# Trunk with a mixture of experts: the fold of the up rows and of the gate rows one half later in each expert pass, with the work that reads them one slot later

## The chip, the cores and the metric

The kernel runs on one core of one Trainium2 chip. The metric is the device time of one execution in microseconds. Its engines are PE (TensorE, matrix products), ACT (ScalarE), DVE (VectorE), POOL (GpSimd) and SP (SyncE, which here only issues the loads of weights). Each engine works off its own list of instructions in order, and they meet at semaphores.

## What is computed

Two layers over 256 rows of 2048 numbers. Each layer is an attention part with three kinds of heads, which the change doesn't touch, and then a mixture of 16 experts, of which each row takes two:

```python
hg = jnp.einsum('nd,edf->nef', t, wg)
hu = jnp.einsum('nd,edf->nef', t, wu)
act = jax.nn.silu(hg) * hu * combine[:, :, None].astype(t.dtype)
out = jnp.einsum('nef,efd->nd', act, wd)
```

For one expert, gate `wg` and up `wu` are 2048 x 512 and down `wd` is 512 x 2048, all in 32-bit floats.

## The kernel before

**Passes.** The experts of a layer are worked off in 16 passes of `step`. Pass k multiplies the gathered rows of expert k by its gate and up weights, and the gated rows of expert k-1 by its down weights. The weights of a pass come as 24 *halves* of 128 x 1024. `PLAN[False]`, written out by hand, is their order: `gggguuggddggdduudduudduu`, halves 0 to 23, g for gate, u for up, d for down. So halves 0 to 7 are gate and up alone, and the first down half is half 8. Pass 0 has no down halves and another order (`PLAN[True]`). After pass 15 come the down halves of the last expert alone.

**A half.** SP loads the weights in pieces of two halves into a ring of 8 buffers (`raw`, and `proj`, which is free in this part). For half h, ACT copies it to a rounded *high* part (`wh`, `cut` on ACT, L555), DVE subtracts this from the half to make the *low* part (`wl`, `cut` on DVE, L1157), and PE multiplies both. `wh` and `wl` have four buffers each (`CUT = 4`), so ACT starts half h only when PE is through with half h-4 (semaphore `cut_free`). A gate or up half is four matrix products on PE (`up_half`, L971 and L973), a down half six (`down_half`, L987 to L989).

**Extra work at slots.** All four engines run the same loop over h, and extra work stands behind the half of a slot: after `cut(h)` on ACT and DVE, after half h on PE. PE is up to four halves behind the cuts, so slot h of ACT and DVE lies earlier in time than slot h of PE. For the up rows of expert k-1, whose last half is half 23 of the pass before, the pass begins with this chain:

- ACT, slot 3 (`UP_OUT`): `up_out` copies the up rows out of their bank (L739).
- PE, slot 1 (`UP_TURN`): `turn_act` folds the two halves of the partitions and turns them, into bank 6 (L962).
- DVE, slot 4: `gated` multiplies them with the gate (L1594).
- ACT, slot 5: `act_hi` makes the high part, two instructions (L744).
- DVE, slot 6: `act_lo` makes the low part (L1600).
- PE: `down_half` of half 8 waits for it.

In between, ACT also stores the last expert's finished rows (`store`, L752), at slots 1, 2, 4 and 6. At slot 6 the store stands behind whatever the slot has of `act_hi`.

The gate rows of expert k have the like chain later in the pass: `gate_out` on ACT at slot 15 (L731), the fold on PE behind half 13 (`GATE_TURN`), `gate_sigmoid` on ACT at slot 17 (L735), `gate_silu` on DVE at slot 19 (L1588). In slots 17 and 22 ACT and DVE also move the turned rows of the next expert (`rows_hi`, L726, and `rows_lo`, L1583).

Of the kernel before, what the change touches and what calls it, by code (L numbers as in the profile page):

```python
# [139 lines left out]
PLAN = {True: "g" * PART + "u" * PART, False: "gggguuggddggdduudduudduu", None: "d" * PART}  # L140
GATED_AT = {first: PLAN[first].rindex("g") for first in (False, True)}
GATE_OUT = {first: at + CUT for first, at in GATED_AT.items()}
GATE_TURN = {first: at + 2 for first, at in GATED_AT.items()}
UP_OUT = CUT - 1
UP_TURN = 1
LAST = NE - 2
JOIN_BANK = (0, 6, 0, 2)
STORE = {PLAN[False].rindex("d") + CUT - 3 * PART + k: n for n, k in enumerate((0, 1, 3, 5))}
# [159 lines left out]
def trunk(nc, x_in, in_units, forget_w, out_units, expert_units, norms, small_in, const_in, router_in,  # L308
          rows_dram, picks_dram, out):
    with ExitStack() as ctx:  # L310
# [231 lines left out]
        def _(e):  # L542
# [6 lines left out]
            def cut(h, slots=RAW, first=0):  # L549

                j = (first + h // 2) % slots
                if h % 2 == 0:
                    e.wait_ge(S[f"raw_landed{j}"], t_.due(f"raw_landed{j}", 16))
                e.wait_ge(S["cut_free"], t_.due("cut_free"))
                act_(wh[:, h % CUT, :], ring[j][:, h % 2 * HALF:(h % 2 + 1) * HALF], ACT.Copy)\  # L555
                    .then_inc(S["hi_ready"], 1)
# [25 lines left out]
            with t_.layers():  # L582
# [141 lines left out]
                def rows_hi(b, g, m=7):  # L724
                    e.wait_ge(S["xt_banked"], t_.due("xt_banked"))
                    act_(stacked[b][:, 8 * g:8 * g + 8, 0:SLOTS],  # L726
                         bank[m][:, :].rearrange("p (c n) -> p c n", n=SLOTS), ACT.Copy).then_inc(S["xt_hi"], 1)

                def gate_out():

                    act_(wide_act, bank[0][:, :], ACT.Copy).then_inc(S["gate_out"], 1)  # L731

                def gate_sigmoid():
                    e.wait_ge(S["gate_turned"], t_.due("gate_turned"))
                    act_(gate_act, bank[6][:, 0:4 * SLOTS], ACT.Sigmoid).then_inc(S["sigmoid"], 1)  # L735

                def up_out():

                    act_(wide_act, bank[1][:, :], ACT.Copy).then_inc(S["up_out"], 1)  # L739

                def act_hi(places=(STACK, 0)):
                    e.wait_ge(S["act_ready"], t_.due("act_ready"))
                    for at in places:
                        ins = act_(actT[:, :, at:at + SLOTS], act.rearrange("p (c n) -> p c n", n=SLOTS), ACT.Copy)  # L744
                    ins.then_inc(S["act_hi"], 1)

                def store(b, k, n):

                    if k == 0:

                        e.wait_ge(S["out_free"], t_.due("out_free"))
                    ins = act_(expert_out[b][:, k * COLS:(k + 1) * COLS], bank[2 + k][0:SLOTS, :], ACT.Copy,  # L752
                               scale=slots[0:SLOTS, bass.ds(n, 1), 2:3].rearrange("p a b -> p (a b)"))
                    if k == 3:
                        ins.then_inc(S["out_ready"], 1)
# [8 lines left out]
                def step(b, k, first=False, last=False, stores=True):  # L764
                    at = 0 if first or b == 1 else 4
                    for h in range(len(PLAN[first])):
                        cut(h, DEEP, at)
                        if h == CUT - 1 and first:
                            for g in range(2):
                                rows_hi(0, g, (7, 5)[g])  # L770
                        if h == UP_OUT and not first:
                            up_out()
                        if h == UP_OUT + 2 and not first:
                            act_hi()
                        if h == GATE_OUT[first]:
                            gate_out()
                        if h == GATE_OUT[first] + 2:
                            gate_sigmoid()
                        if h in XT_MOVE[first] and not last:
                            rows_hi(1 - b, XT_MOVE[first][h])  # L780
                        if h in STORE and stores:
                            store(b, STORE[h], k - 2)
# [27 lines left out]
        def _(e):  # L810
# [147 lines left out]
            def turn_act(at, out, turned):  # L958

                e.wait_ge(S[out], t_.due(out))  # L960
                for k in range(F // P):
                    last = mm(bank[6][:, at + k * SLOTS:at + (k + 1) * SLOTS], wide_act[:, k * P:(k + 1) * P],  # L962
                              cst("fold"), start=True, stop=True)
                last.then_inc(S[turned], 1)
# [27 lines left out]
            def list_slots(experts):  # L992

                if experts[0] in (0, FIRST):
                    e.wait_ge(S["chosen_ready"], t_.due("chosen_ready"))
                for k in experts:
                    for t in range(NT):
                        last = mm(bank[4][0:SLOTS, 4 * k:4 * k + 4], chosen[:, t, k, :], info[:, t, k, :],
                                  start=(t == 0), stop=(t == NT - 1))
                if experts[-1] == NE - 1:  # L1000
                    pair = [chosen[:, t, LAST:NE, :].rearrange("p n s -> p (n s)") for t in range(NT)]
                    for t in range(NT):
                        mm(bank[4][:, 4 * NE:4 * NE + 4], pair[t], info[:, t, NE - 1, :], start=(t == 0),
                           stop=(t == NT - 1))
                    for t in range(NT):
                        last = e.transpose(bank[4][:, (1 + t) * P:(2 + t) * P], pair[t], ident)
                if experts[-1] in (FIRST - 1, NE - 1):
                    last.then_inc(S["slot_banked"], 1)
# [12 lines left out]
            def step(b, first=False, last=False):  # L1021
                for h, part in enumerate(PLAN[first]):
# [5 lines left out]
                    if first and h in LISTED:  # L1028
                        list_slots(LISTED[h])
                    if h == UP_TURN and not first:  # L1030
                        turn_act(4 * SLOTS, "up_out", "up_turned")
                    if h == GATE_TURN[first]:
                        turn_act(0, "gate_out", "gate_turned")
# [115 lines left out]
        def _(e):  # L1149
# [4 lines left out]
            def cut(h, slots=RAW, first=0):  # L1154

                e.wait_ge(S["hi_ready"], t_.due("hi_ready"))
                v.tensor_tensor(wl[:, h % CUT, :],  # L1157
                                ring[(first + h // 2) % slots][:, h % 2 * HALF:(h % 2 + 1) * HALF],
                                wh[:, h % CUT, :].bitcast(F32), ALU.subtract).then_inc(S["lo_ready"], 1)
# [73 lines left out]
            with t_.layers() as layer:  # L1233
# [346 lines left out]
                def rows_lo(b, g, m=7):  # L1580
                    e.wait_ge(S["xt_hi"], t_.due("xt_hi"))
                    k = slice(8 * g, 8 * g + 8)
                    v.tensor_tensor(stacked[b][:, k, SLOTS:STACK], bank[m][:, :].rearrange("p (c n) -> p c n", n=SLOTS),  # L1583
                                    stacked[b][:, k, 0:SLOTS].bitcast(F32), ALU.subtract).then_inc(S["xt_lo"], 1)
# [19 lines left out]
                def choose(a, b):  # L1604
                    v.tensor_tensor(chosen[:, :, a:b, :],
                                    cst("slot").unsqueeze(1).unsqueeze(1).to_broadcast([P, NT, b - a, SLOTS]),
                                    route[:, 3, :, a:b].unsqueeze(3).to_broadcast([P, NT, b - a, SLOTS]),
                                    ALU.is_equal).then_inc(S["chosen_ready"], 1)
# [64 lines left out]
                def step(b, first=False, last=False):  # L1673
                    at = 0 if first or b == 1 else 4
                    for h in range(len(PLAN[first])):
                        cut(h, DEEP, at)
                        if h == CUT - 1 and first:
                            for g in range(2):
                                rows_lo(0, g, (7, 5)[g])
                            choose(FIRST, NE)  # L1680
                        if h == TABLES and first:
                            tables(FIRST, NE)
                            last_tables()
                            ask_again()
                        if h == UP_OUT + 1 and not first:
                            gated()
                        if h == UP_OUT + 3 and not first:
                            act_lo()
                        if h == GATE_OUT[first] + 4:
                            gate_silu()  # L1690
                        if h in XT_MOVE[first] and not last:
                            rows_lo(1 - b, XT_MOVE[first][h])
# [96 lines left out]
```

## Time and profile before

| | before |
|---|---|
| time, three runs | 2103.24, 2096.21, 2102.95 us (median 2102.95) |
| time of the profiled execution | 2098.91 us |
| its span, first to last instruction | 2097.2 us |
| mean granted PE clock over the span | 0.96 |
| busy share of PE, DVE, ACT | 91%, 76%, 69% |
| experts of layer 0 and of layer 1 | about 520 to 1050 us and 1560 to 2097 us |

The span is that of the profiled execution. The shares are means over attention and experts; what one pass of the experts looks like must be read from that stretch alone.

### The profile page before, as it was taken

Reading aid. Unit: us, or ns where it says so; the run is one execution under the profiler, and the core shown is the slowest. Engines: PE = TensorE matmul, PEld = TensorE weight load, DVE = VectorE, ACT = ScalarE, POOL = GpSimd, SP = SyncE. Lnnn points to the kernel's source line nnn. Section 1 sums busy time; section 2 is a strip of 40 time slices with the busy share of each in tenths; the row PEclk is TensorE's granted clock in tenths of the full one; section 3 lists DMA queues with packets and bytes.
Section 4 is the critical chain, followed back from the end, with each engine's and each line's share of the span. In section 5 each row is a group of like instructions: output and inputs, shape, how many; then the busy total and the mean of one; then the engine's idle time right before and its main releaser. Section 6 shows DMA issues by size and latency. Waiting matters only on the chain.

```text
span 2097.2 us, 31165 instructions
## 1 busy us (share of the span) xinstructions
PE 1910.0 (91%) x9018; PEld 1498.3 (71%) x9018; DVE 1600.9 (76%) x2274; ACT 1436.9 (69%) x2276; POOL 91.0 (4%) x86
## 2 busy tenths in 40 slices
PE   6999999995999999999879998999959999999997
PEld 5877777884676777777668777878747777777775
DVE  4567667545999999999855576675469999999997
ACT  4465665442889889889554655654348889888894
POOL 0000000000000001000000000000010001000000
PEclk9999999995999999999889999999969999999998
DMA  8434344553999999999854343444559999999995
GB/s 322 161 141 158 144 143 158 179 204 128 369 404 400 398 405 404 406 393 421 327 184 147 147 155 136 151 151 181 201 181 381 405 405 400 409 397 393 407 407 204
DMA packets 82877, 582.24 MB, mean 278 GB/s; under 512 B 11662, under 2 KB 11918, under 8 KB 13166
## 3 DMA queue, kind: packets, MB, share of 16 engines
q1 hardware_dynamic: 75600, 542.01, 66.5%
q0 software_dynamic: 7168, 38.94, 5.3%
q8 instruction: 48, 0.79, 0.1%
q14 instruction: 61, 0.50, 0.1%
HBM read 575.91 MB, written 29.36 MB: 289 GB/s over the span
## 4 chain that ended last, share of the span: by engine, by line
PE 65%; issue 11%; ACT 11%; DVE 10%; DMA 2%; ACTq 0%; DVEq 0%; SPq 0%; POOLq 0%
PE bank L818 9%; PE bank L820 9%; PE bank L819 9%; PE bank L987 6%; ACT wh L555 6%; PE bank L971 6%; PE bank L989 6%; PE bank L988 6%; PE bank L973 5%; DVE wl L1157 3%; PE bank L954 2%; ACT rows L752 1%; PE bank L962 1%; ACT wide L656 1%; ACT wT L739 1%
## 5 line engine op out<-in xcount | busy, mean ns | idle before, releaser
L1157 DVE TENSOR_TENSOR wl<-raw,wh 128x1024 fp32r<-128x1024 f32 x640 | 766.7, 1222 | 329.7 <-ACT wh L555 329.0
L555 ACT ACTIVATE wh<-raw 128x1024 fp32r<-128x1024 f32 x640 | 664.1, 1054 | 420.0 <-PE bank L820 339.3
L1157 DVE TENSOR_TENSOR wl<-proj,wh 128x1024 fp32r<-128x1024 f32 x384 | 455.4, 1222 | 52.3 <-ACT wh L555 51.9
L971 PE MATMUL bank<-wh,xh 128*128 128x512 f32 x1024 | 430.1, 420 | 34.1 <-DVE wl L1157 31.1
L555 ACT ACTIVATE wh<-proj 128x1024 fp32r<-128x1024 f32 x384 | 394.8, 1052 | 75.7 <-PE bank L989 53.4
L818 PE MATMUL bank<-wh,xh 128*128 128x512 f32 x1024 | 418.2, 408 | 12.5 <-DVE wl L1157 8.7
L973 PE MATMUL bank<-wl,xh 128*128 128x512 f32 x1024 | 408.1, 399 | 0.0
L820 PE MATMUL bank<-wh,xl 128*128 128x512 f32 x1024 | 403.6, 394 | 0.0
L819 PE MATMUL bank<-wl,xh 128*128 128x512 f32 x1024 | 403.0, 394 | 0.0
L971 PEld LDWEIGHTS bank<-wh,xh 128*128 128x128 f32 x1024 | 195.6, 191 | 121.4 <-DVE wl L1157 81.2
L818 PEld LDWEIGHTS bank<-wh,xh 128*128 128x128 f32 x1024 | 195.2, 191 | 58.2 <-DVE wl L1157 14.2
L820 PEld LDWEIGHTS bank<-wh,xl 128*128 128x128 f32 x1024 | 194.6, 190 | 43.5
L819 PEld LDWEIGHTS bank<-wl,xh 128*128 128x128 f32 x1024 | 195.3, 191 | 36.5
L973 PEld LDWEIGHTS bank<-wl,xh 128*128 128x128 f32 x1024 | 196.3, 192 | 34.6
L987 PE MATMUL bank<-wh,actT 128*128 128x512 f32 x512 | 210.7, 412 | 3.7 <-DVE actT L1600 3.7
L988 PE MATMUL bank<-wl,actT 128*128 128x512 f32 x512 | 204.4, 399 | 0.0
L989 PE MATMUL bank<-wh,actT 128*128 128x512 f32 x512 | 204.1, 399 | 0.0
L987 PEld LDWEIGHTS bank<-wh,actT 128*128 128x128 f32 x512 | 97.3, 190 | 38.8 <-DVE wl L1157 11.2
L989 PEld LDWEIGHTS bank<-wh,actT 128*128 128x128 f32 x512 | 97.6, 191 | 23.4
L988 PEld LDWEIGHTS bank<-wl,actT 128*128 128x128 f32 x512 | 97.7, 191 | 19.9
L962 PEld LDWEIGHTS bank<-const,wT 128*128 128x128 f32 x512 | 66.1, 195 | 43.8 <-ACT wT L739 40.4
L962 PE MATMUL bank<-const,wT 128*128 128x64 f32 x512 | 69.1, 279 | 27.2 <-ACT wT L739 27.2
(228 smaller groups left out, 1574.9 us busy)
## 6 DMA issues: line engine op xcount, KB each, us to landing
raw<-in_expert_units SPq DMA_DIRECT2D x192, 1024.0 KB, 9.7
proj<-in_expert_units SPq DMA_DIRECT2D x192, 1024.0 KB, 9.6
raw<-in_in_units SPq DMA_DIRECT2D x96, 1024.0 KB, 4.8
raw<-in_out_units SPq DMA_DIRECT2D x32, 1024.0 KB, 4.8
expert_rows<-rows POOLq DMA_DIRECT2D x4, 1024.0 KB, 4.1
proj<-picks POOLq DMA_DIRECT2D x4, 1024.0 KB, 6.1
x<-in_x SPq DMA_DIRECT2D x2, 1024.0 KB, 6.8
wide<-in_norms POOLq DMA_DIRECT2D x2, 1024.0 KB, 5.0
```

The costliest lines, as they stand in the source:

```text
L555: act_(wh[:, h % CUT, :], ring[j][:, h % 2 * HALF:(h % 2 + 1) * HALF], ACT.Copy)\
L818: mm(out, xh[:, at, tok], rh, start=start, stop=False)
L819: mm(out, xh[:, at, tok], rl, start=False, stop=False)
L820: return mm(out, xl[:, at, tok], rh, start=False, stop=stop)
L954: last = e.transpose(bank[m][:, c * SLOTS:(c + 1) * SLOTS], gathered[b][:, at:at + P], ident[0:SLOTS, 0:SLOTS])
L962: last = mm(bank[6][:, at + k * SLOTS:at + (k + 1) * SLOTS], wide_act[:, k * P:(k + 1) * P], cst("fold"), start=True, stop=True)
L971: mm(bank[m][:, :], stacked[b][:, 2 * h + c, :], wh[:, j, k], start=(h + c == 0), stop=False)
L973: last = mm(bank[m][:, :], stacked[b][:, 2 * h + c, :], wl[:, j, k], start=False, stop=(h == PART - 1 and c == 1))
L987: mm(o, actT[:, k, 0:STACK], wh[:, j, r], start=(k == 0), stop=False)
L988: mm(o, actT[:, k, 0:STACK], wl[:, j, r], start=False, stop=False)
L989: last = mm(o, actT[:, k, SLOTS:SLOTS + STACK], wh[:, j, r], start=False, stop=(k == 3))
L1157: v.tensor_tensor(wl[:, h % CUT, :], ring[(first + h // 2) % slots][:, h % 2 * HALF:(h % 2 + 1) * HALF], wh[:, h % CUT, :].bitcast(F32), A ...
```

## The change

The fold of the up rows moves on PE from behind half 1 to behind half 2, and that of the gate rows from behind half 13 to behind half 14. `gated`, `act_hi` and `act_lo` move one slot later (4 to 5, 5 to 6, 6 to 7), as do the sigmoid (17 to 18) and `gate_silu` (19 to 20). The copies `up_out` and `gate_out` stay where they are. Pass 0 (`first`) and the tail behind pass 15 stay as they were. Nothing is added or taken away.

```diff
 GATE_OUT = {first: at + CUT for first, at in GATED_AT.items()}
-GATE_TURN = {first: at + 2 for first, at in GATED_AT.items()}
+LATER = {True: 0, False: 1}
+GATE_TURN = {first: at + 2 + LATER[first] for first, at in GATED_AT.items()}
 UP_OUT = CUT - 1
-UP_TURN = 1
+UP_TURN = 2
...
# scalar (ACT), step
                         if h == UP_OUT and not first:
                             up_out()
-                        if h == UP_OUT + 2 and not first:
+                        if h == UP_OUT + 3 and not first:
                             act_hi()
                         if h == GATE_OUT[first]:
                             gate_out()
-                        if h == GATE_OUT[first] + 2:
+                        if h == GATE_OUT[first] + 2 + LATER[first]:
                             gate_sigmoid()
...
# vector (DVE), step
-                        if h == UP_OUT + 1 and not first:
+                        if h == UP_OUT + 2 and not first:
                             gated()
-                        if h == UP_OUT + 3 and not first:
+                        if h == UP_OUT + 4 and not first:
                             act_lo()
-                        if h == GATE_OUT[first] + 4:
+                        if h == GATE_OUT[first] + 4 + LATER[first]:
                             gate_silu()
```

The added line shifts every later line number by one, so L744 of before is L745 in the changed kernel. On ACT, from the cut of half 5 to that of half 7, the order before is this (the `L225 ISA` and `REGISTER_ALU` rows are waits on semaphores and their arithmetic; `wh<-` is a cut, `rows<-` a store):

```order
L555 ACTIVATE wh<-proj 128x1024
L225 ISA
L744 ACTIVATE actT<-qkT 128x4x64 x2
L225 ISA
L554 REGISTER_ALU
L555 ACTIVATE wh<-proj 128x1024
L752 ACTIVATE rows<-bank,qkT 64x512
L554 REGISTER_ALU
L555 ACTIVATE wh<-proj 128x1024
```

With the change (the rows are of one pass of the two in the loop; in the other `proj` and `raw` stand the other way round, which makes no difference here):

```order
L556 ACTIVATE wh<-proj 128x1024
L226 ISA
L555 REGISTER_ALU
L556 ACTIVATE wh<-proj 128x1024
L226 ISA
L745 ACTIVATE actT<-qkT 128x4x64 x2
L753 ACTIVATE rows<-bank,qkT 64x512
L555 REGISTER_ALU
L556 ACTIVATE wh<-proj 128x1024
```

The pair `actT<-qkT` (`act_hi`) now stands behind the cut of half 6 instead of ahead of it, and still ahead of the last store and the cut of half 7. On DVE, from `gated` (`qkT<-wT,bank`) to the cut of half 8, the order before is this:

```order
L1594 TENSOR_TENSOR qkT<-wT,bank 128x256
L1156 REGISTER_ALU
L1157 TENSOR_TENSOR wl<-proj,wh 128x1024
L1156 REGISTER_ALU
L1157 TENSOR_TENSOR wl<-proj,wh 128x1024
L1598 REGISTER_ALU
L1600 TENSOR_TENSOR actT<-qkT,actT 128x4x64
L1156 REGISTER_ALU
L1157 TENSOR_TENSOR wl<-proj,wh 128x1024
L1156 REGISTER_ALU
L1157 TENSOR_TENSOR wl<-raw,wh 128x1024
```

With the change, from the cut of half 5 on:

```order
L1158 TENSOR_TENSOR wl<-proj,wh 128x1024
L1593 REGISTER_ALU
L1594 REGISTER_ALU
L1595 TENSOR_TENSOR qkT<-wT,bank 128x256
L1157 REGISTER_ALU
L1158 TENSOR_TENSOR wl<-proj,wh 128x1024
L1157 REGISTER_ALU
L1158 TENSOR_TENSOR wl<-proj,wh 128x1024
L1599 REGISTER_ALU
L1601 TENSOR_TENSOR actT<-qkT,actT 128x4x64
L1157 REGISTER_ALU
L1158 TENSOR_TENSOR wl<-raw,wh 128x1024
```

`gated` now stands behind the cut of half 5, and `act_lo` (`actT<-qkT,actT`) behind that of half 7, directly ahead of the cut of half 8.

On PE, half 1 of a pass, the fold of the up rows (`bank<-const,wT`) and the first product of half 2 before:

```order
L968 REGISTER_ALU
L971 MATMUL bank<-wh,xh 128x512
L973 MATMUL bank<-wl,xh 128x512
L971 MATMUL bank<-wh,xh 128x512
L973 MATMUL bank<-wl,xh 128x512
L960 REGISTER_ALU
L962 MATMUL bank<-const,wT 128x64 x4
L968 REGISTER_ALU
L971 MATMUL bank<-wh,xh 128x512
```

With the change, half 2, the fold and the first product of half 3:

```order
L969 REGISTER_ALU
L972 MATMUL bank<-wh,xh 128x512
L974 MATMUL bank<-wl,xh 128x512
L972 MATMUL bank<-wh,xh 128x512
L974 MATMUL bank<-wl,xh 128x512
L961 REGISTER_ALU
L963 MATMUL bank<-const,wT 128x64 x4
L969 REGISTER_ALU
L972 MATMUL bank<-wh,xh 128x512
```

The fold now has half 2 ahead of it and half 3 behind it. The gate fold moves in the same way behind half 14.

## Rows read from the trace of the kernel before

**Rows 1.** The page, busy time and share of the whole span by engine
```profile
PE 1910.0 (91%) x9018; PEld 1498.3 (71%) x9018; DVE 1600.9 (76%) x2274; ACT 1436.9 (69%) x2276; POOL 91.0 (4%) x86
```

**Rows 2.** Windows, one pass: us, busy of each engine, PE clock, DMA share, GB/s
```profile
730.97:763.35 32.38, 30.72 (x145) 23.26 (x144) 30.18 (x29) 28.90 (x36) 2.63 (x2) 1.00 1.01 403
```

**Rows 3.** Timeline of ACT: start us, us, line, op, out<-in, count [idle <-releaser]
```profile
727.12 1.06 ACT L555 ACTIVATE wh<-raw 128x1024 fp32r<-128x1024 f32 x1 [0.28 <-PE bank L989]
...
731.12 0.58 ACT L739 ACTIVATE wT<-bank 128x512 f32<-128x512 f32 x1
...
733.12 1.06 ACT L555 ACTIVATE wh<-raw 128x1024 fp32r<-128x1024 f32 x1
734.27 0.73 ACT L744 ACTIVATE actT<-qkT 128x256 fp32r<-128x256 f32 x2
734.90 1.05 ACT L555 ACTIVATE wh<-raw 128x1024 fp32r<-128x1024 f32 x1
...
736.42 1.05 ACT L555 ACTIVATE wh<-raw 128x1024 fp32r<-128x1024 f32 x1
737.37 1.05 ACT L555 ACTIVATE wh<-proj 128x1024 fp32r<-128x1024 f32 x1
```

**Rows 4.** Timeline of DVE in the same pass
```profile
732.68 1.23 DVE L1157 TENSOR_TENSOR wl<-raw,wh 128x1024 fp32r<-128x1024 f32 x1 [0.20 <-ACT wh L555]
733.83 0.41 DVE L1594 TENSOR_TENSOR qkT<-wT,bank 128x256 f32<-128x256 f32 x1
734.21 1.23 DVE L1157 TENSOR_TENSOR wl<-raw,wh 128x1024 fp32r<-128x1024 f32 x1
735.99 1.22 DVE L1157 TENSOR_TENSOR wl<-raw,wh 128x1024 fp32r<-128x1024 f32 x1 [0.55 <-ACT wh L555]
737.13 0.42 DVE L1600 TENSOR_TENSOR actT<-qkT,actT 128x256 fp32r<-128x256 f32 x1
737.50 1.22 DVE L1157 TENSOR_TENSOR wl<-raw,wh 128x1024 fp32r<-128x1024 f32 x1
738.64 1.22 DVE L1157 TENSOR_TENSOR wl<-proj,wh 128x1024 fp32r<-128x1024 f32 x1
```

**Rows 5.** Timeline of PE in the same pass
```profile
730.60 0.40 PE L973 MATMUL bank<-wl,xh 128*128 128x512 f32 x1
731.76 1.10 PE L962 MATMUL bank<-const,wT 128*128 128x64 f32 x8 [0.76 <-ACT wT L739]
...
737.26 0.50 PE L971 MATMUL bank<-wh,xh 128*128 128x512 f32 x1 [0.57 <-DVE wl L1157]
...
739.92 0.50 PE L987 MATMUL bank<-wh,actT 128*128 128x512 f32 x1
```

**Rows 6.** Waits, 565 to 1020 us: us in total, times, longest us
```profile
ACT wh L555 <- PE bank L989: 37.5, 86, 1.1
...
DVE wl L1157 <- ACT wh L555: 30.4, 70, 0.7
...
PE bank L962 <- ACT wT L739: 10.8, 14, 0.8
```

**Rows 7.** Waits of SP's queue, 560 to 1040 us
```profile
SPq L437 <- DVE wl L1157: 344.9, 166, 2.9
```

**Rows 8.** Timeline of ACT around the sigmoid, one pass earlier
```profile
716.10 1.06 ACT L555 ACTIVATE wh<-proj 128x1024 fp32r<-128x1024 f32 x1 [1.11 <-PE bank L989]
717.06 0.36 ACT L735 ACTIVATE wT<-bank 128x256 f32<-128x256 f32 x1
...
717.92 1.06 ACT L555 ACTIVATE wh<-proj 128x1024 fp32r<-128x1024 f32 x1
```

**Rows 9.** Timeline of ACT, then of DVE, at the start of pass 1
```profile
539.94 0.73 ACT L744 ACTIVATE actT<-qkT 128x256 fp32r<-128x256 f32 x2 [1.43 <-DVE qkT L1594]
...
539.49 0.42 DVE L1594 TENSOR_TENSOR qkT<-wT,bank 128x256 f32<-128x256 f32 x1
...
541.65 1.23 DVE L1157 TENSOR_TENSOR wl<-raw,wh 128x1024 fp32r<-128x1024 f32 x1 [0.61 <-ACT wh L555]
```

## The prediction

> **What bounds the kernel now.** I began with the page. PE is busy 91% of the span [rows 1], but its records overlap, so this doesn't say that PE sets the pace. The change acts on the expert passes alone, so I took one pass by itself, fold to fold. It lasts 32.38 us, with ACT busy 28.90, DVE 30.18, the granted PE clock at 1.00 and the DMA engines at their full share with 403 GB/s [rows 2]. Four resources are close to full, and the question is which wait ends last, and where.
>
> The waits of a stretch of passes say this. ACT waits for PE (86 times, 37.5 us), DVE for ACT (70 times, 30.4 us), and PE for `up_out` before the up fold: 14 times, 10.8 us in all, so 0.77 each [rows 6]. That last wait is the one the moved fold would take away. It occurs in the 14 passes 2 to 15. SP's queue waits for DVE to free a buffer, 344.9 us in some 480 [rows 7], and no wait of ACT for a landing is among the long ones.
>
> Then I went through the start of one pass, in order of time. ACT's cut of half 1 waits for PE (0.28) at 727.12. From there ACT runs almost without a pause: half 1, a store, and so on to `up_out` at 731.12, the cut of half 5 at 733.12, `act_hi` at 734.27, half 6 at 734.90, the last store and half 7 at 736.42, half 8 at 737.37 [rows 3]. DVE waits for ACT's half 6 and cuts it at 735.99, then `act_lo` at 737.13, half 7 at 737.50, half 8 at 738.64 [rows 4]. PE's half 8 begins at 739.92 [rows 5], which is the 1.22 us of DVE's cut of half 8 and 0.06 behind its start. So from 727.12 to 739.92, 12.80 us, the path runs over ACT and then DVE. The other 19.6 us of the pass are PE's halves 8 to 21, until PE lets ACT go again at half 1. PE's own wait at the fold lies inside the first stretch, beside that path and not on it: after it, PE is out of work again and waits 0.57 at 737.26 for the low part of half 6 [rows 5].
>
> **The change, part by part.**
>
> *Up fold behind half 2.* `up_out` starts at 731.12 and takes 0.58, so its rows are there at 731.70. PE's last record of half 1 ends at 731.00 (730.60 + 0.40), and the fold starts at 731.76 [rows 3, 5]. Half 2 now goes into that hole of 0.76, and the fold behind it finds its rows. Halves 3 to 5 may come up to 0.76 earlier, but only to wait for low parts: DVE cuts half 5 from 734.21 and half 6 from 735.99 [rows 4], at times that PE doesn't set. This part by itself: 0.
>
> *`gated` behind DVE's cut of half 5.* DVE cuts half 4 at 732.68, one cut to the next instruction is 1.15, so it is free at 733.83. The high part of half 5 is ready at 733.12 + 1.06 = 734.18 [rows 3, 4]. The cut of half 5 thus starts at about 734.21, exactly as before, and the slot that `gated` filled stays empty. `gated` starts at 735.35 (734.21 + 1.14) and ends at 735.76 instead of 734.24.
>
> *`act_hi` behind ACT's cut of half 6.* ACT cuts half 6 at 733.12 + 0.95 = 734.07 (0.95 is the distance of the cuts of halves 7 and 8 [rows 3]) and has nothing to do from about 735.1. It must wait for `gated`, at the head of its queue, with the last store and the cuts of halves 7 and 8 behind it. `act_hi` starts at 735.79, 1.52 later than 734.27; half 6 went ahead by 0.95 of that. What stands behind both is late by 1.52 - 0.95 = 0.57. The cut of half 7 starts at 736.42 + 0.57 = 736.99 and is ready at 738.04.
>
> *`act_lo` behind DVE's cut of half 7.* DVE cuts half 6 early, which helps nobody, then waits for half 7 and starts it at 738.07 instead of 737.50. `act_lo` used to lie between halves 6 and 7. It now lies between 7 and 8, on the path, for 0.37 (737.50 - 737.13 [rows 4]). Half 8 starts at 738.07 + 1.14 + 0.37 = 739.58 instead of 738.64, and PE's half 8 at 740.86 instead of 739.92: 0.57 + 0.37 = 0.94 late.
>
> *Does it come back?* Behind half 8 PE sets the pace. ACT's later cuts wait for PE, 0.44 in the mean and 1.1 at most [rows 6], and shift with it. Nothing there runs ahead of PE by more than its four buffers, so the pass becomes 0.94 longer.
>
> *Gate fold, sigmoid, silu.* ACT's cut of half 17 waits 1.11 for half 13 either way; behind it stand the sigmoid at 717.06 and the cut of half 18 at 717.92 [rows 8]. With the sigmoid behind half 18, `rows_hi` and the cut go first. Half 14 is through on PE by then, now even without the fold ahead of it, and PE has the same work in a row. I count 0; the most it could lose is a fold, 1.10 [rows 5], if the sigmoid had to wait for all of it, and the gain would be bounded by the 1.11 that ACT waits before half 17, where PE is the one waited for.
>
> *Pass 1 is different.* It has no stores, so ACT is not the laggard: `act_hi` waits 1.43 for `gated` already, and ACT stands at half 6, ready to go [rows 9]. Before, half 7 on ACT came at 539.94 + 0.63 + 0.95 = 541.52. Now `gated`, 539.49 before, follows a cut of 1.14 and ends at 541.05, `act_hi` takes ACT 0.63 more, to 541.71, and half 7 follows at once: 0.19 later, while the half 6 that DVE had to wait for until 541.65 is done early. I count 0 for this pass.
>
> *Sum.* 14 passes in each of two layers by 0.94 are 26.3 us. Against the profiled execution, 2098.91 us, that is 2125.2. The three other runs shown are 2103.24, 2096.21 and 2102.95; the mean of the four is 2101.3, and 2101.3 + 26.3 = 2127.6. I say 2128. Bounds of the term: the least is 0.57 a pass, where DVE has room for `act_lo` (16 us, 2117); the most is 0.94 and a second `act_lo` slot of 0.37 with it, 1.31 (37 us, 2138).
>
> The pass moved 403 GB/s with the DMA engines at full share [rows 2], which speaks for a bound by loads; that SP's queue waits for buffers [rows 7] speaks against it. The Trainium skill, Perfetto Trace Analysis, Identifying the Most-Contended Engine with Engine Utilization, measures DMA by its rate against 358 GB/s for one core; by that rule the DMA, at 113%, would be the most contended here, ahead of DVE and ACT, a delay on these two would disappear, and the sum would be 0. The trace doesn't agree, since the engines don't wait for landings.
>
> **The rivals.**
>
> *A: it gets faster.* The 0.77 us wait before the fold goes and PE keeps the lead. If PE's progress from half 0 to 7 set the time of half 8, the hole of 0.76 would be saved in 28 passes, -21 us, 2080. For it: it is PE's wait with one releaser in every pass, seen in all 14 [rows 6]. Against it: PE waits again at halves 6 and 7 for DVE. It decides only if DVE's low part of half 8 is ready before PE gets there, and even now PE starts half 8 only 0.06 behind it [rows 4, 5]. The Trainium skill, Perfetto Trace Analysis, Optimization Strategies, speaks for this rival: when PE is idle waiting for others, free it.
>
> *B: no difference.* Loads set the pace of a pass, 32.4 us, and shorter or longer work of the engines inside it is hidden: 2101. For it: the full DMA share [rows 2]. Against it: [rows 7], and that ACT's waits are for PE [rows 6]. In the same place falls that ACT and DVE catch up from half 9 to 21; against that, their waits there are for PE, which is late itself.
>
> *C: slower, but by the 0.57 alone*, or less, because DVE's order absorbs `act_lo`: 2117. It needs DVE to be ahead at half 7, and it is not, since half 7 starts as soon as ACT has it.
>
> **How the numbers follow.** My forecast, 0.94 a pass, gets 0.66; C 0.12; A 0.12; B 0.10. A measurement of this kernel can tell about 0.5%, 10.5 us. The first two are both slower by more than that: slower 0.78, within 0.5% 0.10, faster 0.12. The range takes in C and the upper bound with 3 us to either side for the spread of the runs shown: 2112 to 2140.
>
> **What the changed kernel's profile would show.** A pass of about 33.3 us. PE's wait for `up_out` gone. ACT idle about 0.7 us ahead of `act_hi`, released by `gated`, in passes 2 to 15. DVE idle about 0.4 ahead of half 5 and 1.2 ahead of half 7. PE waiting about 1 us longer before half 7, which needs the low part that is late, and reaching half 8 behind `act_lo` and its cut. The stretch around the sigmoid as before. I would be wrong if ACT's cuts of halves 7 and 8 didn't move behind `act_hi`, if a pass stayed at 32.4 with those waits in it (B), or if PE's half 8 came earlier in a pass (A).

## The result, and the profile after

The changed kernel took 2123.59 us (median of 4 runs, 2119.66 to 2128.16), the kernel before 2102.27 (4 runs, 2096.21 to 2103.24). The ratio is 1.0108, with a 95% interval of 1.0079 to 1.0137: slower by about 23 us, where +26 us was forecast (the two medians lie 21.3 us apart). The time lies 4 us below the 2128 of the forecast, inside its range of 2112 to 2140. The kernel `up_only` below, which differs from it only in the gate chain, gives 1.0130 (1.0082 to 1.0178).

The windows view, one pass, fold to fold, with the columns of [rows 2]:

```profile
604.77:638.07 33.30, 31.18 (x145) 23.18 (x145) 30.16 (x29) 28.86 (x36) 2.66 (x2) 1.00 1.00 392
```

33.30 us instead of 32.38, with the same busy time of ACT and DVE: the engines do the same work and stand idle 0.9 us more. The PE clock is 1.00 in both. All 13 full passes (2 to 14) of either layer have this length, 33.29 to 33.31. Pass 15, which has no transposes for a next expert, went from 30.69 to 31.59. Fourteen passes in two layers by 0.91 are 25.5 us. The two profiled spans differ by 29.3 us (2126.5 against 2097.2). The rest lies outside these passes; 2.3 us of it was there before the first pass began (`up_out` of pass 1 at 537.77 against 535.47), where no instruction was moved.

The timeline of ACT in the changed kernel, from `up_out` to the cut of half 8 (lines are one higher; the row with x2 is the cuts of halves 5 and 6):

```profile
604.77 0.58 ACT L740 ACTIVATE wT<-bank 128x512 f32<-128x512 f32 x1
...
606.76 2.01 ACT L556 ACTIVATE wh<-raw 128x1024 fp32r<-128x1024 f32 x2
609.44 0.73 ACT L745 ACTIVATE actT<-qkT 128x256 fp32r<-128x256 f32 x2 [0.68 <-DVE qkT L1595]
610.08 0.67 ACT L753 ACTIVATE rows<-bank,qkT 64x512 f32<-64x512 f32 x1
610.64 1.04 ACT L556 ACTIVATE wh<-raw 128x1024 fp32r<-128x1024 f32 x1
611.59 3.89 ACT L556 ACTIVATE wh<-proj 128x1024 fp32r<-128x1024 f32 x4
```

Against [rows 3]: half 6 is cut right behind half 5, then ACT stands for 0.68 us at `act_hi`, released by DVE's `gated`. The store and half 7 come behind it. From `up_out` to the cut of half 7 it was 5.30 us (731.12 to 736.42), and now it is 5.87 (604.77 to 610.64): 0.57 later.

The timeline of DVE in the same pass, from the cut of half 4 to that of half 8 (the last row is halves 8 to 11):

```profile
606.33 1.22 DVE L1158 TENSOR_TENSOR wl<-raw,wh 128x1024 fp32r<-128x1024 f32 x1 [0.20 <-ACT wh L556]
607.86 1.23 DVE L1158 TENSOR_TENSOR wl<-raw,wh 128x1024 fp32r<-128x1024 f32 x1 [0.30 <-ACT wh L556]
609.00 0.41 DVE L1595 TENSOR_TENSOR qkT<-wT,bank 128x256 f32<-128x256 f32 x1
609.33 1.22 DVE L1158 TENSOR_TENSOR wl<-raw,wh 128x1024 fp32r<-128x1024 f32 x1
611.72 1.23 DVE L1158 TENSOR_TENSOR wl<-raw,wh 128x1024 fp32r<-128x1024 f32 x1 [1.18 <-ACT wh L556]
612.87 0.42 DVE L1601 TENSOR_TENSOR actT<-qkT,actT 128x256 fp32r<-128x256 f32 x1
613.20 4.63 DVE L1158 TENSOR_TENSOR wl<-proj,wh 128x1024 fp32r<-128x1024 f32 x4
```

Against [rows 4]: DVE idles 0.30 ahead of half 5, and 1.18 ahead of half 7 (it was 0.55, ahead of half 6). Then `act_lo` stands between halves 7 and 8. Measured from `up_out`, half 8 starts at 8.43 (613.20 - 604.77), where it was 7.52 (738.64 - 731.12): 0.91 later.

The timeline of PE: the fold, the first product of halves 5, 6 and 7, and half 8:

```profile
605.70 1.00 PE L963 MATMUL bank<-const,wT 128*128 128x64 f32 x8
...
609.14 0.50 PE L972 MATMUL bank<-wh,xh 128*128 128x512 f32 x1 [0.34 <-DVE wl L1158]
...
610.60 0.50 PE L972 MATMUL bank<-wh,xh 128*128 128x512 f32 x1 [0.28 <-DVE wl L1158]
...
613.00 0.50 PE L972 MATMUL bank<-wh,xh 128*128 128x512 f32 x1 [1.21 <-DVE wl L1158]
...
614.48 0.50 PE L988 MATMUL bank<-wh,actT 128*128 128x512 f32 x1 [0.27 <-DVE wl L1158]
```

Against [rows 5]: the fold waits for nothing. The wait of 0.76 is gone. Behind it PE now waits 0.34, 0.28, 1.21 and 0.27 us for low parts from DVE, 2.10 us together. Before, it waited 0.57 there at half 6 [rows 5] and this at half 7:

```profile
738.78 0.50 PE L971 MATMUL bank<-wh,xh 128*128 128x512 f32 x1 [0.33 <-DVE wl L1157]
```

The waits view over the passes of the changed kernel says the same:

```profile
DVE wl L1158 <- ACT wh L556: 42.3, 83, 1.2
ACT wh L556 <- PE bank L990: 41.0, 81, 1.1
PE bank L972 <- DVE wl L1158: 25.6, 42, 1.2
...
ACT actT L745 <- DVE qkT L1595: 9.4, 14, 0.7
```

`PE <- ACT L739` of [rows 6] is no longer there; ACT's wait for `gated`, 14 times 0.67, is new.

### The profile page after: what moved, and what is told of

Read it like the earlier page. It is cut to its first block, busy times and chain, and to the rows that moved or that the text cites. A ratio compares the mean times of both kernels' runs of the same rounds, so it can differ in the third digit from the quotient of the medians.

```text
span 2126.5 us, 31165 instructions
## 1 busy us (share of the span) xinstructions
PE 1926.3 (91%) x9018; PEld 1497.4 (70%) x9018; DVE 1600.7 (75%) x2274; ACT 1436.7 (68%) x2276; POOL 91.4 (4%) x86
## 4 chain that ended last, share of the span: by engine, by line
PE 62%; ACT 13%; issue 11%; DVE 10%; DMA 2%; ACTq 1%; DVEq 0%; SPq 0%; POOLq 0%
PE bank L819 9%; PE bank L821 9%; PE bank L820 8%; ACT wh L556 7%; PE bank L988 6%; PE bank L990 6%; PE bank L989 5%; PE bank L972 5%; PE bank L974 4%; DVE wl L1158 3%; ACT rows L753 3%; PE bank L955 2%; PE bank L963 1%; ACT wide L657 1%; ACT wT L740 1%
## 5 line engine op out<-in xcount | busy, mean ns | idle before, releaser
L974 PEld LDWEIGHTS bank<-wl,xh 128*128 128x128 f32 x1024 | 197.1, 193 | 32.2
L753 ACT ACTIVATE rows<-bank,qkT 64x512 f32<-64x512 f32 x120 | 80.1, 669 | 0.0
L491 POOL DMA_INDIRECT proj<-expert_rows,tok_at x32 | 53.4, 1668 | 526.6 <-PE bank L955 436.0
```

The source lines that it names most:

```text
L491: e.indirect_dma_start(gathered[k % 2], None, rows_dram[:, :], bass.IndirectOffsetOnAxis(ap=tok_at[0:SLOTS, k % NE, :], axis=0), bounds_ch ...
L974: last = mm(bank[m][:, :], stacked[b][:, 2 * h + c, :], wl[:, j, k], start=False, stop=(h == PART - 1 and c == 1))
```

## The experiments

The length of a pass is the distance between two starts of `up_out` in ACT's timeline, which is the same to some 0.05 us in all full passes of a kernel unless said otherwise. The ratios, with their 95% intervals, compare whole executions with those of the kernel before on the same chip.

| kernel | full pass, us | against 32.39 | ratio, 95% interval |
|---|---|---|---|
| before | 32.39 | | |
| changed | 33.30 | +0.91 | 1.0108 (1.0079 to 1.0137) |
| gate_only | 32.40 | 0 | 1.0007 (0.9982 to 1.0032) |
| up_only | 33.30 | +0.91 | 1.0130 (1.0082 to 1.0178) |
| fold_only | 32.39 | 0 | 0.9986 (0.9961 to 1.0011) |
| lo_back | 32.97 | +0.58 | 1.0066 (1.0042 to 1.0091) |
| store_first | 32.75 | +0.36 | 1.0060 (1.0040 to 1.0079) |
| gated_back | 32.53 | +0.14 | 1.0022 (1.0000 to 1.0045) |
| one_more | 32.40 | 0 | 0.9999 (0.9978 to 1.0021) |
| hi_later | 32.18 | -0.21 | 0.9992 (0.9973 to 1.0011) |
| best | 31.59, three late passes up to 34.6 | -0.80 | 0.9986 (0.9965 to 1.0007) |
| best_cols | 31.60 | -0.79 | 0.9907 (0.9876 to 0.9937) |

### Which half of the change: gate_only and up_only

gate_only has the gate chain moved and the up chain as before; up_only the other way round. gate_only undoes all edits of the up chain (`UP_TURN`, `gated`, `act_hi`, `act_lo`); up_only is the changed kernel with this edit:

```diff
-LATER = {True: 0, False: 1}
+LATER = {True: 0, False: 0}
```

> Only the gate fold, the sigmoid and the silu move, the up chain is as before. My theory (ACT's and DVE's queues at the start of a pass carry the loss): a pass stays at 32.4 us, fold to fold, and the time is that of before within 0.3%. Rival (the gate fold and the sigmoid are what costs): all of the 0.91 us a pass, about +1.1%.

> Only the up chain moves, the gate chain is as before. My theory: a pass of 33.3 us, as in the changed kernel, about +1.1%. Rival (the gate fold is the cause): 32.4 us and no difference.

gate_only's passes have 32.40 us, up_only's 33.30. So the up chain carries the whole loss. In two passes of up_only, one in each layer, 1.0 and 1.5 us came on top. Its trace shows what they are: right behind PE's wait of 1.22 us for the low part of half 7 (up to 707.67 in layer 0, to 1695.69 in layer 1) the granted PE clock is at its lower level, 1.2 GHz, for some 3 us (0.53 of full speed from 707.60 to 711.20, 0.50 from 1697.80 to 1701.00), and PE's products start 0.43 us apart there instead of 0.23. The other passes have the same wait and the clock at 1.00; why it fell in these two isn't shown.

In the changed kernel the stretch around the sigmoid runs as worked out. Its ACT timeline, cut of half 17, `rows_hi`, cut of half 18, sigmoid:

```profile
589.73 1.06 ACT L556 ACTIVATE wh<-proj 128x1024 fp32r<-128x1024 f32 x1 [1.07 <-PE bank L990]
590.70 0.58 ACT L727 ACTIVATE xh<-bank 128x512 fp32r<-128x512 f32 x1
591.17 1.05 ACT L556 ACTIVATE wh<-proj 128x1024 fp32r<-128x1024 f32 x1
592.12 0.37 ACT L736 ACTIVATE wT<-bank 128x256 f32<-128x256 f32 x1
```

Nothing waits there but half 17, for PE, 1.07 us (1.11 in [rows 8]).

### PE's fold alone: fold_only

The kernel before with the up fold behind half 2 and everything on ACT and DVE in its old slot:

```diff
-UP_TURN = 1
+UP_TURN = 2
```

> Only PE's up fold goes behind half 2; gated, act_hi and act_lo stay in their slots. My theory: PE's wait of 0.77 us for up_out goes, the fold ends before DVE reaches gated, and the pass stays at 32.4 us: no difference. Rival A (PE's wait before the fold is on the path): 31.6 us a pass, about -1.0%. A third way: the later fold makes gated wait and costs up to 0.9 us a pass.

No difference. The timeline of PE, the fold and the first products of halves 5, 6 and 7:

```profile
602.59 1.00 PE L962 MATMUL bank<-const,wT 128*128 128x64 f32 x8
...
606.03 0.50 PE L971 MATMUL bank<-wh,xh 128*128 128x512 f32 x1 [0.33 <-DVE wl L1157]
...
607.80 0.50 PE L971 MATMUL bank<-wh,xh 128*128 128x512 f32 x1 [0.58 <-DVE wl L1157]
...
609.32 0.50 PE L971 MATMUL bank<-wh,xh 128*128 128x512 f32 x1 [0.32 <-DVE wl L1157]
```

The wait of 0.76 ahead of the fold is gone, and PE waits at half 5 instead (0.33, none before). Its half 5 starts 4.37 us behind `up_out` (606.03 - 601.66), where it was 4.40 (735.52 - 731.12): what PE gained at the fold is used up by then. It was slack of PE's, not time of the pass. This settles rival A.

### The two terms apart: lo_back and store_first

lo_back is the changed kernel with `act_lo` back in slot 6, where DVE stands idle:

```diff
-                        if h == UP_OUT + 4 and not first:
+                        if h == UP_OUT + 3 and not first:
                             act_lo()
```

> The changed kernel with act_lo alone put back to slot 6, ahead of DVE's cut of half 7, where DVE stands idle. My theory (0.57 from the wait of ACT for gated, 0.37 from act_lo ahead of half 8): 0.37 a pass less than the changed kernel, so 32.95 us a pass and +0.7 to +0.8% against before. Rival (act_lo costs nothing, ACT's wait is all): 33.3 us.

32.97: 0.33 less. Its DVE timeline, half 6, `act_lo`, half 7:

```profile
606.12 1.22 DVE L1158 TENSOR_TENSOR wl<-raw,wh 128x1024 fp32r<-128x1024 f32 x1
607.25 0.41 DVE L1601 TENSOR_TENSOR actT<-qkT,actT 128x256 fp32r<-128x256 f32 x1
608.51 1.23 DVE L1158 TENSOR_TENSOR wl<-raw,wh 128x1024 fp32r<-128x1024 f32 x1 [0.84 <-ACT wh L556]
```

`act_lo` now lies in the hole ahead of half 7, of which 0.84 is left. What remains is the delay from ACT's wait, 0.58 a pass.

store_first is the changed kernel with the last store a slot earlier, ahead of the cut of half 6:

```diff
-STORE = {... for n, k in enumerate((0, 1, 3, 5))}
+STORE = {... for n, k in enumerate((0, 1, 3, 4))}
```

> The changed kernel with the last store of slot 6 moved to slot 5 of ACT, ahead of the cut of half 6, so that ACT has work while it waits for gated. My theory: ACT's cut of half 7 is back at its old time, only act_lo ahead of DVE's half 8 is left, 32.75 to 32.8 us a pass, about +0.5% against before. Rival (what counts is how late gated and act_hi are, not what stands behind them): 33.3 us.

32.75. Its ACT timeline, the store, half 6, `act_hi`, half 7 (`up_out` starts at 599.20):

```profile
602.15 0.68 ACT L753 ACTIVATE rows<-bank,qkT 64x512 f32<-64x512 f32 x1
602.72 1.06 ACT L556 ACTIVATE wh<-raw 128x1024 fp32r<-128x1024 f32 x1
603.87 0.73 ACT L745 ACTIVATE actT<-qkT 128x256 fp32r<-128x256 f32 x2
604.50 1.04 ACT L556 ACTIVATE wh<-raw 128x1024 fp32r<-128x1024 f32 x1
```

`act_hi` is as late as in the changed kernel (4.67 us behind `up_out` in both), but the store fills the wait, and half 7 follows `act_hi` at its old time (5.30 behind `up_out`). Only the term of `act_lo` is left, 0.36. The two kernels' remainders, 0.58 and 0.36, make 0.94 together; the changed kernel's loss is 0.91.

### Is it the lateness of the chain: gated_back and one_more

gated_back is the changed kernel with `gated` in its old slot; fold, `act_hi` and `act_lo` stay late:

```diff
-                        if h == UP_OUT + 2 and not first:
+                        if h == UP_OUT + 1 and not first:
                             gated()
```

> The changed kernel with gated alone put back to slot 4, behind the fold that stands behind half 2. My theory: ACT finds gated done and doesn't wait, which even wins it the 0.2 us that it waited before the change; act_lo ahead of half 8 costs its 0.37; together about +0.17: 32.55 us a pass, +0.2%. Rival (the late fold is the cause): 33.3 us.

one_more moves `gated` and `act_hi` by yet another slot, to 6 and 7:

```diff
-                        if h == UP_OUT + 3 and not first:
+                        if h == UP_OUT + 4 and not first:
                             act_hi()
...
-                        if h == UP_OUT + 2 and not first:
+                        if h == UP_OUT + 3 and not first:
                             gated()
```

> The changed kernel with gated and act_hi another slot later (6 and 7), act_lo still in slot 7. My theory: ACT's last store and cut of half 7 now stand ahead of act_hi and fill the wait, act_lo falls into the time in which DVE waits for ACT's half 8: 32.4 us a pass, as before the change, though the chain is later still. Rival (the later the chain, the longer the pass): 34 us or more.

gated_back: 32.53. With `gated` early, ACT doesn't wait, though the fold is behind half 2. The +0.14 is near the 0.36 of `act_lo` less the 0.2 that ACT waited for `gated` before the change, the move that hi_later below makes alone. one_more: 32.40, the whole loss gone, with the chain later than ever. Its ACT timeline, halves 5 and 6, the last store, half 7, `act_hi`, half 8 and on:

```profile
603.43 2.00 ACT L556 ACTIVATE wh<-raw 128x1024 fp32r<-128x1024 f32 x2
605.33 0.68 ACT L753 ACTIVATE rows<-bank,qkT 64x512 f32<-64x512 f32 x1
605.89 1.06 ACT L556 ACTIVATE wh<-raw 128x1024 fp32r<-128x1024 f32 x1
607.24 0.72 ACT L745 ACTIVATE actT<-qkT 128x256 fp32r<-128x256 f32 x2 [0.29 <-DVE qkT L1595]
607.87 3.89 ACT L556 ACTIVATE wh<-proj 128x1024 fp32r<-128x1024 f32 x4
```

ACT still waits for `gated`, 0.29, but the store and half 7 are ahead of it. This is the run that shows the mechanism best: what costs is not when the chain is done, as long as half 8 has it in time, but what stands in the queue behind the instruction that waits.

### What follows from it: hi_later and best

hi_later is the kernel before with `act_hi` alone a slot later, so that it no longer waits 0.2 us for `gated`:

```diff
-                        if h == UP_OUT + 2 and not first:
+                        if h == UP_OUT + 3 and not first:
                             act_hi()
```

best has this too, and the first and the last store out of the stretch in which ACT runs without a pause:

```diff
-STORE = {... for n, k in enumerate((0, 1, 3, 5))}
+STORE = {... for n, k in enumerate((-1, 1, 3, 6))}
```

> The kernel before with act_hi alone one slot later (5 to 6), the one of the changed kernel's moves that takes ACT's 0.2 us wait for gated away. Theory: 0.2 us a pass less, 32.2 us, -0.25% at most, if the loads, which run at 404 GB/s already, keep up with it; rival: the loads hold it at 32.4.

> Not the change but what follows from it: the kernel before with act_hi behind the cut of half 6 (slot 6), gated, act_lo and the fold as they were, and the first and the last store at slots 0 and 7, where ACT waits for PE or runs ahead. My theory (ACT's work from half 1 to half 8 is on the path): about 0.8 us a pass less, 31.6 us, -1.0%. Rival B (the loads set the pace of a pass): 32.4 us, no difference.

hi_later's passes have 32.18 us, 0.21 less, in both layers. One of them, pass 13 of layer 0, has 32.26; there ACT waits twice for a load to land, 0.7 us in all. In the time of the whole kernel 6 us don't stand out of the spread. best is where my expectation failed: -1.0% was expected, -0.14% was measured, no difference that the runs can tell. Its passes 2 to 10 have, in both layers, the 31.6 us that I had worked out. Passes 11 to 13 have 33.98, 34.64 and 34.42 in layer 0 and 32.83, 33.71 and 33.42 in layer 1; pass 14 has 31.6 again. In the two profiled executions best is still 9.3 us shorter than the kernel before over passes 1 to 15 of both layers, and 8.1 us longer in the rest, attention above all. Two windows of best, ahead of the long passes and in them:

```profile
824.00:855.00 31.00, 30.28 (x143) 23.26 (x144) 29.50 (x29) 28.30 (x35) 2.62 (x2) 1.00 1.01 407
889.00:924.00 35.00, 31.24 (x145) 23.16 (x144) 30.13 (x30) 29.14 (x37) 2.09 (x2) 1.00 1.01 389
```

The waits of best in the late stretch:

```profile
ACT wh L555 <- DMA raw<-in_expert_units: 6.8, 5, 2.7
...
ACT wh L555 <- DMA proj<-in_expert_units: 3.5, 6, 1.3
```

No such wait is among those of the kernel before. These are 10.3 us in 850 to 960 us of layer 0; the three passes there are 8.3 us longer together than at 31.6 each. The DMA view of best shows where they come from. q0 is the queue of POOL's gather and scatter, with what it moved in MB and its share of the DMA engines' time; the row under it is the loads' median time to landing. First from 571 to 850 us, then from 855 to 960 us, there with the rate in 40 slices of 2.6 us:

```profile
q0 software_dynamic: 1365, 4.03, 4.6%
raw<-in_expert_units SPq DMA_DIRECT2D x52, 1024.0 KB, 10.9
...
GB/s 297 424 421 415 431 415 428 421 421 424 421 371 212 331 415 421 421 428 421 428 418 424 424 415 375 187 259 412 428 418 424 421 421 424 412 437 409 424 415 421
q0 software_dynamic: 433, 2.11, 7.0%
raw<-in_expert_units SPq DMA_DIRECT2D x19, 1024.0 KB, 19.2
```

The rate is 409 to 437 GB/s but for three dips, down to 187. They go with the gathers that POOL issues at 847.52, 881.16 and 915.43: the second and third begin some 3 us behind the issue, and all are over when the gather has landed (10.1 us in the median). Such a dip stands in the earlier passes too, and in those of the kernel before. It is wider where POOL's queue moves more: about 3 us in pass 3 of layer 0 (0.42 MB), 6 us in pass 12 (0.92 MB). So the loads lose lead: in layer 0 of best a piece lands 8.3 us behind its issue in pass 2 and 19.2 us behind it in pass 11. The lead is eight buffers at most, and then ACT waits. In the kernel before the same time grows from 8.4 us in pass 2 to 13.6 us in pass 12, and ACT doesn't wait yet. In pass 12 of layer 0, best moved 13.5 MB at 390 GB/s, which are the 34.6 us of that pass; the kernel before moved 12.7 MB in it and lived on its lead. That the gather makes these passes the heavy ones is read from the times of the dips; no run changes the gather alone.

### Are the loads what holds it: best_light, before_light, best_cols

best_light is best, and before_light the kernel before, with one in eight of the experts' pieces loaded for 64 of 128 partitions only, a sixteenth less in all. The other rows of the piece stay stale, so these two don't compute the reference.

```diff
+p = P // 2 if slots == DEEP and j == DEEP - 1 else P
-e.dma_start(ring[j], units[bass.ds(at + j, 1)].rearrange("o p n -> (o p) n"))\
+e.dma_start(ring[j][0:p, :], units[bass.ds(at + j, 1)].rearrange("o p n -> (o p) n")[0:p, :])\
```

> The kernel with the shorter ACT stretch (31.58 us in its early passes, 34 in late ones), with one in eight of the experts' weight pieces loaded for 64 of its 128 partitions, so that the other 64 rows of that piece are stale: the output isn't the reference's, the work of the engines is the same, the loads of a pass are a sixteenth less. Theory now (the loads run out of rate in the late passes): 31.6 us in all passes, about 20 us less than the kernel before, -1.0%. Rival (something else in the late passes, such as POOL's indirect transfers): the late passes of 34 us stay.

> The kernel before with the same sixteenth of the experts' weights left unloaded (output not the reference's). Theory (queues of ACT and DVE at the start of a pass set the 32.4 us, loads don't): 32.4 us a pass, no difference. Rival B (loads set the pace): a sixteenth less, 30.4 us a pass, or down to the 31.6 that the engines allow: faster by 1% or more.

Neither theory foresaw this: both got slower, 1.0609 (1.0564 to 1.0654) and 1.0665 (1.0587 to 1.0743), with passes from 31.6 to 46 us. DMA of before_light in the passes:

```profile
DMA packets 18798, 129.85 MB, mean 325 GB/s; under 512 B 2948, under 2 KB 2948, under 8 KB 2948
...
raw<-in_expert_units SPq DMA_DIRECT2D x63, 1024.0 KB, 20.8
...
proj<-in_expert_units SPq DMA_DIRECT2D x15, 512.0 KB, 21.6
```

Fewer bytes, but 325 GB/s instead of the 403 of [rows 2], and 21 us from issue to landing of a whole piece. With the half-partition loads in between, the whole queue is slower, and ACT waits for landings, 77.0 us in 565 to 1045 us of before_light. So these runs say nothing on the question; they only show what the kernel looks like when loads do set the pace.

best_cols is best and leaves out as much in another shape: all 128 partitions, half of the columns (again not the reference's result):

```diff
+n = HALF if slots == DEEP and j == DEEP - 1 else UNIT
+e.dma_start(ring[j][:, 0:n], units[bass.ds(at + j, 1)].rearrange("o p n -> (o p) n")[:, 0:n])\
```

> The kernel with the shorter ACT stretch, with one in eight of the experts' weight pieces loaded for all 128 partitions but only its first 1024 of 2048 columns (the other half of the piece is stale, so the output isn't the reference's; all engines' work is the same). The half-partition loads ran the queue at 312 GB/s and can't be read as fewer loads; these keep all partitions. Theory (the loads run out of rate in the late passes at 31.6 us): 31.6 us in every pass and -1.0% against before. Rivals: late passes stay at 33 to 34 us with ACT's waits for landings gone (another cause), or half loads cost the queue its rate in this shape too and the passes get longer than 32.4.

31.6 us in all 13 full passes of both layers (31.58 to 31.62), 0.9907 (0.9876 to 0.9937). DMA of best_cols and its time to landing:

```profile
DMA packets 23749, 156.35 MB, mean 391 GB/s; under 512 B 3443, under 2 KB 3443, under 8 KB 5888
...
raw<-in_expert_units SPq DMA_DIRECT2D x75, 1024.0 KB, 7.4
proj<-in_expert_units SPq DMA_DIRECT2D x57, 1024.0 KB, 8.1
```

At 391 GB/s a piece lands within 7 to 8 us and ACT never waits for one, with POOL's transfers as in best. The engines' part of best is thus as worked out, and what broke its gain off is that the loads fell behind. No kernel here that does the full work is clearly faster than the kernel before.

## Why the prediction was right

**The path.** That it runs over ACT and DVE from the cut of half 1 to PE's half 8, and over PE from there on, is what all the pass lengths agree with: fold_only takes a PE wait away for nothing, while hi_later takes 0.2 us off ACT and shortens the pass by 0.21.

**Up fold behind half 2: 0.** fold_only: 0.00 a pass.

**ACT's wait for `gated`: 0.57.** lo_back, which has this term alone, 0.58; in the trace half 7 is cut 0.57 later.

**`act_lo` ahead of half 8: 0.37.** The one term of the sum that was off, by little: 0.36 in store_first, but 0.33 between lo_back and the changed kernel. [Rows 4] show 0.37 from `act_lo` to the next cut; in the changed kernel it is 0.33 (612.87 to 613.20). So 0.91, not 0.94, and 25.5 us, not 26.3.

**The start and the range.** The mean of the four times before is 2100.3 (2098.91, 2103.24, 2096.21, 2102.95), not 2101.3, so the sum should have read 2126.6. And 3 us beyond 2117 and 2138 are 2114 and 2141, not 2112 and 2140. Neither slip changes the outcome.

**Gate chain: 0.** gate_only: 0.00 a pass, 1.0007.

**Pass 1: 0.** 33.70 us against 33.68 in layer 0. In layer 1 it is 33.69 against 32.68, but fold_only has the 33.7 there too, without any move on ACT or DVE, and the kernel before has it in layer 0, so I don't put it down to the change.

**It doesn't come back.** From half 8 on, ACT's first wait, at half 12, is 0.70 us instead of 0.35, since PE was delayed by more than ACT; the later ones are as before (1.07 at half 17 in both), and no pass got any of the 0.91 back.

**Rival A** (the wait ahead of the fold is worth 0.76 a pass): refuted by fold_only. **Rival C** (0.57 alone): refuted by store_first, where `act_lo` costs with no wait on ACT.

**Rival B** (loads set the pace) was refuted for this change, since a pass got longer by all that ACT and DVE lost. But I dismissed it more than the rows allowed. The full DMA share of [rows 2] did mean something: a little below the 32.4 us of the pass the loads do come in. hi_later's 32.2 held, with two short waits for landings in one pass; best's 31.6 held in passes 2 to 10. A rival that says "this resource is the bound" can be wrong for a change that makes the pass longer and right for one that makes it shorter. The rule of the Trainium skill (Perfetto Trace Analysis, Identifying the Most-Contended Engine) names the engine or queue to improve first, which by its rate is the DMA here. What the prediction made of it, that a delay of the others would disappear, the runs refute (33.30 us). As a rule of what to improve it is borne out in part: 0.21 us a pass was won on ACT alone, and the 0.8 us of best did not hold in all passes until there were fewer bytes to load.

## What to carry to other kernels

When work is moved in a static order across engines, work out for each instruction that may wait what stands behind it in its queue; a later slot may cost, and a slot later still may cost nothing. The wait that the profile shows on the busiest engine may be slack: see what that engine waits for next, once it is gone. And before taking the gain of a shorter pass, see how the loads' time to landing develops from pass to pass: where it grows, lead is being used up, and the pass with the most other transfers decides.

## What was not expected of the hardware

Loading 64 instead of 128 partitions in one of eight pieces brought the DMA rate from 403 GB/s [rows 2] to 325 GB/s and the landing of a whole piece to 21 us, while loading half of the columns did no harm (391 GB/s with 7 to 8 us to landing, where the kernel asked for no more). No run here tells why.

The limit of the loads is not one rate of a pass. The mean was 407 GB/s over passes 2 to 10 of best in layer 0, 4 more than in [rows 2], and its loads fell behind; in pass 14 of layer 0 the kernel before moved 423. Outside the gather's dips the slices show 409 to 437 GB/s, inside them down to 187, and how much of a pass the dips take differs from pass to pass. Why the rate falls by more than half during the gather, no run here tells.
